# A causal convolution of 31 taps shared by three engines: third block of channels, six lower halves of weights and the order of the queries' stage changed

## What is computed

```python
def conformer_conv(u, conv_dw, conv_dw_b, conv_ln_g, conv_ln_b, w_conv_pw):
    a, gate = jnp.split(u, 2, axis=-1)
    h = a * jax.nn.sigmoid(gate)
    h = lax.conv_general_dilated(
        h, conv_dw[:, None, :].astype(h.dtype), window_strides=(1,),
        padding=[(CONV_WIDTH - 1, 0)],
        dimension_numbers=("NWC", "WIO", "NWC"),
        feature_group_count=D_CONV) + conv_dw_b
    h = jax.nn.silu(layer_norm(h, conv_ln_g, conv_ln_b))
    return h @ w_conv_pw

hn = rms_norm(h, mix_pre_g)
proj = hn @ w_in
q = proj[..., :D_Q].reshape(B, S, N_Q_HEADS, HEAD_DIM)
k = proj[..., D_Q:D_Q + D_KV].reshape(B, S, N_KV_HEADS, HEAD_DIM)
v = proj[..., D_Q + D_KV:D_Q + 2 * D_KV].reshape(B, S, N_KV_HEADS, HEAD_DIM)
u = proj[..., D_Q + 2 * D_KV:]
attn_out = sliding_window_attention(q, k, v, attn_sinks, rel_bias)
conv_out = conformer_conv(u, conv_dw, conv_dw_b, conv_ln_g, conv_ln_b, w_conv_pw)
```

## Time and profile before

| | us |
|---|---|
| median of 3 runs | 2297.38 |
| lowest and highest | 2297.24 and 2298.58 |
| the profiled execution, its time | 2298.58 |
| its span from first to last instruction | 2296.8 |
| TensorE busy in the span | 2264.1 |
| VectorE, ScalarE, GpSimd busy | 1358.5, 1035.4, 1028.3 |

### The profile page before, as it was taken

How to read it: one execution, slowest core, us unless ns; L and a number is a source line. 1 busy time by engine, 2 the same in 40 slices (tenths; PEclk the granted TensorE clock), 3 DMA queues, 4 the chain that set the end, 5 groups by cost and what they waited for, 6 DMA issues and landing times.

```text
span 2296.8 us, 30705 instructions
## 1 busy us (share of the span) xinstructions
PE 2264.1 (99%) x11442; PEld 1889.2 (82%) x11442; DVE 1358.5 (59%) x2182; ACT 1035.4 (45%) x2057; POOL 1028.3 (45%) x900
## 2 busy tenths in 40 slices
PE   8989999999999999999999999999999999999998
PEld 7777788888888888888898878888888888888887
DVE  6996516944444477776533676154584454547776
ACT  6577734433232345456634765135443323234543
POOL 2886535488787700033112022224448878770003
PEclk9999999999999999999999999999999999999999
DMA  6122134233233368664002001143223323336865
GB/s 213 37 74 79 51 115 136 66 115 122 86 125 103 125 244 286 210 217 136 19 10 72 22 12 38 65 169 115 101 82 101 126 85 125 103 115 247 296 210 195
DMA packets 218980, 278.48 MB, mean 121 GB/s; under 512 B 16396, under 2 KB 142988, under 8 KB 215760
## 3 DMA queue, kind: packets, MB, share of 16 engines
q1 hardware_dynamic: 199056, 212.81, 29.3%
q10 hardware_dynamic: 19776, 63.71, 7.0%
HBM read 208.30 MB, written 68.17 MB: 120 GB/s over the span
## 4 chain that ended last, share of the span: by engine, by line
PE 89%; POOL 3%; DVE 3%; ACT 2%; issue 1%; DMA 1%; ACTq 0%; POOLq 0%; SPq 0%; DVEq 0%
PE P L513 26%; PE P L515 26%; PE P L514 26%; PE P L3242 3%; POOL acc L1315 2%; PE P L3261 2%; PE P L3277 2%; PE P L3199 1%; PE P L525 1%; PE P L4408 1%; PE P L1602 1%; PE P L4390 0%; DVE P L1242 0%; DVE P L1235 0%; ACT wh L473 0%
## 5 line engine op out<-in xcount | busy, mean ns | idle before, releaser
L513 PE MATMUL P<-ah,wh 128*128 128x512 f32 x1120 | 440.3, 393 | 10.6 <-DVE wl L479 5.2
L515 PE MATMUL P<-ah,wl 128*128 128x512 f32 x1120 | 437.0, 390 | 0.0
L514 PE MATMUL P<-al,wh 128*128 128x512 f32 x1120 | 436.7, 390 | 0.0
L513 PE MATMUL P<-wh,ah 128*128 128x512 f32 (+2 forms) x1128 | 425.9, 378 | 0.0
L515 PE MATMUL P<-wh,al 128*128 128x512 f32 (+2 forms) x1128 | 423.3, 375 | 0.0
L514 PE MATMUL P<-wl,ah 128*128 128x512 f32 (+2 forms) x1128 | 422.9, 375 | 0.0
L595 POOL TENSOR_TENSOR stats<-stats,epsc 128x1 f32<-128x1 f32 x70 | 27.7, 395 | 633.0 <-ACT xn L2088 421.0
L513 PEld LDWEIGHTS P<-ah,wh 128*128 128x128 f32 x1120 | 210.9, 188 | 57.1 <-issue 6.0
L515 PEld LDWEIGHTS P<-ah,wl 128*128 128x128 f32 x1120 | 210.7, 188 | 44.3
L514 PEld LDWEIGHTS P<-al,wh 128*128 128x128 f32 x1120 | 210.9, 188 | 42.6
L515 PEld LDWEIGHTS P<-wh,al 128*128 128x128 f32 x1128 | 212.2, 188 | 36.9
(11 more groups left out here) (399 smaller groups left out, 4432.0 us busy)
## 6 DMA issues: line engine op xcount, KB each, us to landing
rf<-ff_rows SPq DMA_DIRECT2D x154, 256.0 KB, 5.3
stage<-in_w_down_dram SPq DMA_DIRECT2D x110, 256.0 KB, 3.9
ff_rows<-sb ACTq DMA_DIRECT2D x22, 1024.0 KB, 5.0
stage<-in_w_gu_dram SPq DMA_DIRECT2D x44, 512.0 KB, 5.1
stage<-in_w_gate_dram SPq DMA_DIRECT2D x22, 512.0 KB, 4.2
stage<-in_w_up_dram SPq DMA_DIRECT2D x22, 512.0 KB, 5.2
ff_rows<-uo ACTq DMA_DIRECT2D x22, 512.0 KB, 3.0
stage<-in_w_down_dram SPq DMA_DIRECT2D x22, 512.0 KB, 5.3
```

The source lines that it names most:

```text
L513: e.matmul(out, lh, rh, start=start, stop=False, skip_group_check=onto)
L514: e.matmul(out, lh, rl, start=False, stop=False, skip_group_check=onto)
L515: return e.matmul(out, ll, rh, start=False, stop=stop, skip_group_check=onto)
```

## The change

VectorE takes the whole of block 2, in the same half-length form as 1 and 3; whole taps are gone. GpSimd and ScalarE make block 0 alone, with four buffers of 512 instead of two of 1024, so a product waits for the add four before it. The lower halves of pieces 10 to 15 go to GpSimd: `LOWS_AFTER` puts those of the four pieces of queries behind the adds of index 46, 48, 53 and 58, and two more of the memory follow at the end. In the queries' stage ScalarE makes four products after the first copy of a name and three after the second, and the copies of the turned values stand right behind the second copy of `q0`. VectorE's taps are dealt out anew: 7 and 7 instead of 14 in front of block 2, then 5, 9, 5, 7 instead of 9, 5, 12, with one lower half moved ahead of the last seven, and 12 instead of 14 for each name of the queries' stage. What waited for the last tap of block 2 on GpSimd waits for the last one of block 0.

```diff
-    lows_by_dve = {*range(22), *range(first["chunk"], first["chunk"] + 4), first["co"] + 2, first["co"] + 3}
+    lows_by_dve = {*range(10), *range(16, 22), *range(first["chunk"], first["chunk"] + 4), first["co"] + 2, first["co"] + 3}
...
-    SPLIT = (1, 3)
+    SPLIT = (1, 2, 3)
...
-    tap_products = [sb(f"tap_product{i}", [128, 1024], off["extra"] + 256 + 4 * KB * i) for i in range(2)]
+    tap_products = sb("tap_products", [128, 4, 512], off["extra"] + 256)
...
             if c > 1:
-                DV.wait_ge(tap, ("out", 1, 0) if c == 2 else ("whole", 2, SHARED - 1))
+                DV.wait_ge(tap, ("out", c - 1, 0))
...
-            n -= 1.8 if op[0] == "whole" else 1
+            n -= 1
 
     PRODUCTS = [(0, a, a + 512, w) for a in (0, 512) for w in range(TAPS)]
-    PRODUCTS += [(2, 0, 1024, w) for w in range(SHARED, TAPS)]
...
-                if k >= 2:
-                    c2, a2, _, w2 = ADDED[k - 2]
+                if k >= 4:
+                    c2, a2, _, w2 = ADDED[k - 4]
                     AC.wait_ge(pt, (c2, a2, w2))
...
+    LOWS_AFTER = {46: first["kvq"] + 2, 48: first["kvq"] + 3, 53: first["kvq"] + 4, 58: first["kvq"] + 5}
+
+    def pool_taps():
+        for k, (c, a, b, w) in enumerate(ADDED):
+            PL.wait_ge(ep, (c, a, w))
+            if k:
+                c2, a2, _, w2 = ADDED[k - 1]
+                PL.wait_ge(pt, (c2, a2, w2))
+            PL.e.tensor_tensor(acc[:, c, a:b], acc[:, c, a:b], tap_products[:, k % 4, :], ALU.add).then_inc(
+                *pt.up((c, a, w)))
+            if k in LOWS_AFTER:
+                low_to(LOWS_AFTER[k])
...
-        send_to(c)
+        send_to(c + 1)
         for i, name in enumerate(KVQ):
-            for th in range(2):
-                kv_copy(name, th)
-                if th == 0:
-                    send_to(c + i + 3)
-                some_products(4)
+            kv_copy(name, 0)
+            send_to(c + i + 3)
+            some_products(4)
+            kv_copy(name, 1)
             if name == "q0":
-                for g in range(2):
...
+                values_turned()
+            some_products(3)
+            if name == "q1":
                 AC.wait_ge(l_b1, "all")
...
-        some_taps(14)
+        some_taps(7)
         glu(0, 1)
         low_by_dve_to(5)
         DV.ends("u0")
+        some_taps(7)
         for c in range(2, 4):
-            some_taps(9)
+            some_taps(5)
             gate(c)
             low_by_dve_to(2 * c + 2)
-            some_taps(5)
+            some_taps(9)
             values(c)
             glu(c, 0)
-            some_taps(12)
+            some_taps(5)
+            low_by_dve_to(2 * c + 3)
+            some_taps(7)
             glu(c, 1)
-            low_by_dve_to(2 * c + 3)
             add_taps(c)
-        low_by_dve_to(first["kvq"])
+        low_by_dve_to(first["kvq"] + 1)
         for i, name in enumerate(KVQ):
             rooted(KVQ_BANKS[name][0], (name, 0), mm, (name, 0, 0))
-            some_taps(7)
+            some_taps(6)
             low_by_dve_to(first["kvq"] + min(i, 4) + 3)
-            some_taps(7)
+            some_taps(6)
         DV.ends("q3")
...
-        pool_taps(0)
-        pool_taps(2)
+        pool_taps()
+        low_to(first["mem_k"] + 1)
```

50 lines of the change are left out of this document (14 added, 36 removed).

## The result

| | kernel before | changed kernel |
|---|---|---|
| median time, 21 runs each | 2297.26 us (2296.95 to 2299.0) | 2301.39 us (2297.93 to 2302.38) |
| ratio | | 1.0015, 95% interval 1.0008 to 1.0021 |
| profiled execution: time, span | 2298.58, 2296.8 us | 2302.38, 2300.6 us |
| first attention scores start | 181.72 us | 171.93 us |
| first maxima of VectorE start | 182.37 us | 174.75 us |

By the medians the change costs 4.1 us; the interval of the ratio is 1.8 to 4.8 us. The forecast was 2297.1, which its sum has as 0.3 us less than before: the direction was wrong. The stage of keys, values and queries does end 9.8 us earlier, but 12.6 were forecast, and attention's first steps give back more than that. From the wait for `zl` to the end of the span both kernels take the same: 2296.8 - 282.50 = 2014.3 and 2300.6 - 286.35 = 2014.25 us. So everything happens ahead of that point.

What follows compares the result with a forecast made beforehand. TensorE, busy 2264.1 of 2296.8 us, was taken as the bound. A stage gain of 12.6 us worked down to -1.9, plus 1.6 for the clock, made -0.3; forecast 2297.1 us, range 2294.0 to 2301.5.

Steps and rivals of the forecast that it cites:

- The first three waits go: TensorE's waits for VectorE's lower halves at 63.66, 87.12 and 116.03 vanish, gaining 3.8 us.
- 2.1 us earlier than 69.36: VectorE's third-block gate comes at 67.3 with fewer taps ahead, so GpSimd's second batch starts some 2.0 us earlier.
- A new wait of 1.3 us: Queries' stage: GpSimd's first lower half ends at 124.4, while TensorE wants it at 123.2.
- GpSimd late: Rival, chance 0.13: GpSimd's first lower half ends at 129.4, TensorE waits 6.3 us, lost clock costs 1.6 more; 2303.7.
- Fourth and fifth wait go: TensorE's waits at 142.30 and 158.22 for ScalarE's copies vanish with their slow stretches, 10.1 us; stage ends at 169.1.
- What is late next: VectorE: Taps behind the last queries' scaling delay first maxima to 171.9; 21.2 us of queue ends the memory's scaling at 193.1.
- The clock's 1.6 us at step eight: Attention's step eight: TensorE's wait of some 2.6 us for VectorE's copy brings half speed, costing 1.6 us.
- Half speed throughout: Rival, chance 0.10: TensorE stays at 1.2 GHz from the first maxima on, adding 1.7 us; 2298.8.
- The rule of the Trainium skill, "TensorE: Matmul & The Clock Gate", Part 1: Attention's start: a little-busy array gets half its clock pulses, so the whole sparse stretch would run at half speed.
- Taps covered: Rival, chance 0.07: the 18 taps in attention's first steps fit into VectorE's waits, TensorE's 12.6 us stay; 2284.8.
- The rule on the two engines' shared side: VectorE's two-SBUF-input lower halves and GpSimd instructions exclude each other; both engines win by the move, sum unchanged.
- VectorE's chain -1.9: VectorE's queue to the memory's scaling leaves 1.9 us of the stage's 12.6; the step of 196.30 comes at 194.4.

Runs made afterwards that it cites:

- 11 matmuls: Changed kernel plus 11 matmuls of 128x128, results unread, in TensorE's wait at 125.72 for GpSimd's first lower half: 2300.51 us.
- the run with 16 matmuls: Changed kernel plus 16 matmuls of 128x128, results unread, behind the turns of attention's step eight (pause at 194.62): 2299.64 us.
- all places filled: Changed kernel plus unread matmuls in three places: 11 at 125.7, 10 and 5 behind attention's second and third score tiles, 14 in step eight: 2298.78 us.
- the first edit: Changed kernel with the fourth block's taps dealt otherwise, 15 moved ahead of VectorE's last scaling: 2292.86 us.
- the second: Changed kernel with GpSimd's first lower half two adds earlier: 2298.30 us alone, 2291.99 together with the taps dealt otherwise.

## Why the prediction was wrong, by its steps

In short: two lower halves of VectorE were taken at 1.2 us and took 2.04 and 2.18, so GpSimd's first lower half came 1.2 us later than summed, TensorE waited 2.61 us instead of 1.3, and a lower clock level followed that had been left out of the sum. In the profiled executions the forecast's -0.3 became +3.85 us by that lateness (1.2), that level (1.8) and 0.7 more for the level at step eight; 0.45 stays open.

- **The first three waits go**: right. None is left at the places of the earlier trace rows at 63.66, 87.12 and 116.03.
- **"2.1 us earlier than 69.36", the gate ahead of GpSimd's second batch**: this failed, and it is where the lateness starts. The gate came at 68.38, 1.0 earlier. Ahead of it stands a lower half of VectorE that I took at 1.21 us and that took 2.04, which is 0.8 of the 1.1 us missing; the rest is a longer wait for TensorE at 57.91 (2.18 us, of which an earlier start of the taps gave back 1.4, where 0.5 was allowed in all). The lower half at 82.35 took 2.18, against 1.2 in the sum. From there each step hands it on, as the chain that ended last shows: second batch 71.37 (70.3 forecast), third 96.77 (95.3), ScalarE's table 114.02 (112.5), upper halves done 119.85 (118.5), first lower half done 125.6 (124.4).

```profile
58.18 1.30 POOL L1300 TENSOR_TENSOR acc<-acc,tap_products 128x512 f32<-128x512 f32 x1
58.52 2.04 DVE L479 TENSOR_TENSOR wl<-stage,wh 128x1024 fp32r<-128x1024 f32 x1
59.62 2.09 POOL L1300 TENSOR_TENSOR acc<-acc,tap_products 128x512 f32<-128x512 f32 x1
...
81.88 1.57 POOL L1300 TENSOR_TENSOR acc<-acc,tap_products 128x512 f32<-128x512 f32 x1
82.35 2.18 DVE L479 TENSOR_TENSOR wl<-stage,wh 128x1024 fp32r<-128x1024 f32 x1
```

- **Why 2.04 and not 1.21.** The lines, each from the timeline of its engine, show it. The lower half of 58.52 starts while an add of GpSimd is running, which ends at 59.48; 0.96 us of its 2.04 are over by then and 1.08 follow. The next add, begun at 59.62, takes 2.09 us instead of 1.30. The same sum fits everywhere: rest of the running add, then 1.1 us.

| kernel | lower half starts | add still runs for | sum with 1.1 | took |
|---|---|---|---|---|
| before | 62.30 | 0.06 | 1.2 | 1.21 |
| before | 85.76 | 0.09 | 1.2 | 1.22 |
| before | 96.12 | 0.62 | 1.7 | 1.70 |
| before | 113.70 | 1.10 | 2.2 | 2.18 |
| before | 149.25 | 1.38 | 2.5 | 2.46 |
| changed | 58.52 | 0.96 | 2.1 | 2.04 |
| changed | 82.35 | 1.10 | 2.2 | 2.18 |
| changed | 107.66 | 0.48 | 1.6 | 1.56 |

Over the traces of all sixteen kernels, from 50 to 180 us, it holds for each of the 76 lower halves of VectorE that start during an add of GpSimd, with 1.08 to 1.17 us behind the add's end; the 29 that start with no GpSimd instruction running took 1.20 to 1.23. So the 1.21 at 62.30 was the luck of starting 0.06 us before an add's end, and the trace of the kernel before already had the 2.18 at 113.70. With adds of 1.3 us, 1.44 apart, I estimate from these rows 1.2 to 2.4 us for a half, by where it falls.

- **"A new wait of 1.3 us"**: the mechanism was right, the size was not. It was 2.61, and the level behind it, which I charged only in the rival "GpSimd late", came as well. TensorE resumed at 125.72 and not at 124.5; 1.2 us of lateness and up to 1.8 us of clock were missing from the sum. What I had called decisive from 3 us of lateness on decides from 1.2 on. The run with the half two adds earlier and the one with it on VectorE show this term, wait and level together, at 3.1 and 3.9 us (with what a shorter level at step eight gave in them).
- **Fourth and fifth wait go, 10.1 us**: right. TensorE turns the values without a wait before them, and 158.22 has no counterpart. The stage's end was 171.93 instead of 169.1 by the step above alone (1.2 of lateness and 1.6 of clock; with the clock held by 11 matmuls it is 170.33).
- **"What is late next: VectorE"**: right to 0.1 us. First maxima 2.82 us behind the stage's end (2.8), chain to the scaling's end 21.3 (21.2). Since it stands behind the stage's end, it passed on the 2.8 us: 196.08 against 193.1. Moving the taps and leaving 16 out both show that it is the path.
- **The clock's 1.6 us at step eight**: it came, for 6.6 us and not 3.3; by the run with 16 matmuls it costs 1.75 in the median (2.2 against its own set). In the profiled executions it is 2.3: from the run with 11 matmuls to the one with all places filled, the wait for `zl` moves from 284.59 to 282.32. The stretch was taken too short; that part of it is covered kept the price near.
- **The rivals.** "GpSimd late" (0.13) was the one that happened in kind, with 1.2 us of lateness and not the 5 I worked it out for; 2301.4 lies between the forecast and its 2303.7. "Half speed throughout" had the granted clock right in two stretches of 6.6 us, but the middle one cost nothing. The rule of the Trainium skill, "TensorE: Matmul & The Clock Gate", Part 1, that stood behind it agrees with the trace in that the matmuls that fill the pauses kept the clock at 1.00. "Taps covered" was wrong.
- **The rule on the two engines' shared side.** The Trainium skill, "SBUF — State Buffer", "SBUF: two separate sides", speaks of a VectorE instruction with two SBUF inputs and one of GpSimd that shut each other out. I set it beside the sum as changing nothing. The trace agrees, by its letter: the durations above are those of two instructions of which neither does its work before the other has ended, whichever came first. (The add begun at 71.37, during VectorE's half of 70.71, took 1.73 us instead of 1.30.) It did change the sum: I thought of it for the halves that move to GpSimd and not for those that stay. A tap with one input in PSUM came every 0.66 us beside the same adds, as I had it. The memory's scaling, also with two inputs in SBUF, follows the same rule: 1.28 us in the kernel before, where GpSimd's normalising ran for 0.06 us more, and 1.70 in the changed one, where it ran for 0.62.

The sum by what was measured, in the profiled executions, as changes of the wait for `zl` (282.50 before, 286.35 after, +3.85): VectorE's chain -1.9 as forecast, +1.2 for the later end of the wait, +1.8 for the level behind it (286.35 to 284.59 in the run with 11 matmuls), +2.3 for the level at step eight. That is +3.4, and 0.45 is not placed. The run with all places filled has 282.32, -0.2, against the -1.9 + 1.2 = -0.7 that the sum gives for it, with the same 0.5 open.

In the medians, each against the kernel before of its own set, the levels cost 3.4 us (4.1 for the changed kernel, 0.7 with all places filled): -1.9 + 1.2 + 3.4 = +2.7 of the 4.1. One more step of the forecast bears on the rest. Its -1.9 was read from an execution of the kernel before 1.3 us above the median, and was put on the median. If that 1.3 lay in the stretch that the change speeds up, as one of the two levels of the earlier trace rows would, the median gains 0.6 and not 1.9, and the sum is +4.0. No run shows where the 1.3 lay.

## What to carry to other kernels

When work moves off an engine, look where that engine will be idle and put the remaining work of the same queue there: here the 8.5 us that made the change pay lay in 15 taps of VectorE that could go ahead of its last scaling instead of behind it. An instruction that an in-order engine makes for TensorE must be placed by the first moment at which it can be ready against the moment at which it is wanted, each predecessor priced with its neighbours at work; a margin of 1 us over 60 us of queue is none. A duration read once is not a price: look for the same instruction elsewhere in the trace, and for what ran beside it. Here the two lower halves that I took at 1.2 us, 40 and 65 us upstream, took 1.8 us more between them and made most of the new wait's error. And the gains of two edits add only as long as no engine is full: after the first edit VectorE was, and the second brought 0.9 of its 3.1 us, the 1.1 that VectorE still had idle.

## What was unexpected of the hardware

- A pause of TensorE of 2.4 to 2.7 us was followed by a granted clock of 0.50 for 3.4 us at one place and 6.6 at two others, and at 125.7 us in some executions not at all (2.63 us of pause, clock 1.00). At step eight the stretch behind the same pause was 6.6 us in the changed kernel and under 4 with the first queries' half on VectorE. A level also came behind shorter pauses close together, of 1.15 and 1.47 us, where the taps were dealt otherwise (0.50 in 178 to 180 us). What decides this, no run here tells.
- A matmul of 128x128 in f32 on `causal` shows as two records and takes 0.23 us, so the number of them that fits into a pause is half of what the mean of one record suggests.
- VectorE's lower half of 128x1024, with both inputs in SBUF, took 1.21 to 2.46 us beside the same kind of GpSimd adds, and all of that spread is the rest of the add that runs when it starts; it takes 1.08 us from that add's end, and the add that then wants to start takes 2.09 us instead of 1.30. Taps, with one input in PSUM, came 0.66 us apart all along.
